# Turning the value product of an attention stage round, with V stationary and two heads in two column halves

## The chip, the cores and the metric

The kernel runs on one core of one Trainium2 chip. The metric is the device time of one launch in microseconds, the median of several runs. A core has a matrix engine (TensorE), three engines for elementwise work (VectorE, ScalarE, GpSimd), a DMA-issuing engine (SyncE) and 16 DMA engines. The engines run in parallel and wait for each other on semaphores. TensorE writes its results to PSUM, which has eight banks of 128 partitions x 512 fp32 words; here each bank is a tensor `bank[0]` to `bank[7]`.

## The reference

A trunk of two decoder layers over 512 tokens of width 1024, all in fp32. Layer 0 mixes tokens by sliding-window attention (window 128, 16 query heads of width 64 on 4 key/value heads, one learned sink logit per head), layer 1 by forgetting attention (16 heads, causal, with a bias c[t] - c[s] on the logits). Each is followed by a mixture of 16 experts of which each token uses two. Cut to the part that matters:

```
# layer 0, per head h and block of 128 queries; layer 1 without sink, over all earlier keys
scores = q @ k.T * 64**-0.5            (masked; layer 1: + c[q] - c[k])
probs  = softmax([scores, sink])[..., :-1]
out    = probs @ v                     # 64 columns per head
mix    = concat(out over heads) @ w_o
x      = layer_norm(alpha * x + mix)
```

## The kernel before

Each engine has its own instruction stream, written out by hand; order across engines comes only from named semaphores (`eng.wait_ge(S(name), n)`). Weights come through a ring of four slots in SBUF, loaded by SyncE. Plain fp32 matmuls are used for attention; the projections use three fp32r matmuls each (lines 523 to 525), with operands split in a high and a low part.

The attention of a layer works on 8 pairs of heads (`hp`). A pair has four steps, one for each block of 128 queries `n`, in the order 0, 3, 1, 2 (`N_ORDER`), so a layer has 32 steps `s`. In layer 0 block 0 sees one key tile of 128 keys and the others two; in layer 1 block n sees n + 1 tiles. `half` is the head within the pair. A step consists of:

- `scores(s)` on TensorE (line 618): Q times K for both heads. Head 0's operands lie in partitions 0 to 63 and head 1's in 64 to 127. In layer 1 a bf16 matmul adds the causal mask (line 624).
- `mask_and_max(s, half)` on VectorE (lines 1201 and 1208): adds the bias, scales, takes the maximum and writes to `sp` in SBUF.
- `expo(s, half)` on ScalarE (line 913): the exponential, with the row sums accumulated into `rsum` (the accumulator's read-out is a second record of the line).
- `turn_probs(s)` on TensorE (line 635): one transpose per key tile and head, head 0 into bank 3, head 1 into bank 4.
- `evac_probs(s)`: copies the transposed probabilities to `pT`, head 0 by ScalarE (line 927), head 1 by VectorE (line 1225). There is one `pT` for each head, so the copy of step s waits for the value product of step s - 1.
- `mix(s)` on TensorE (line 652): the value product. The transposed probabilities (128 x 128) are stationary, 64 columns of V move; the output is queries x head width in bank 5 or 6, by the pair's parity.

TensorE's order is, for each s: `turn_probs(s)`, `mix(s - 1)`, `scores(s + 2)`. ScalarE's is `expo(s + 1, 0)`, `evac_probs(s)`, `expo(s + 1, 1)`, and, in some steps, a cast of output weights (line 933). VectorE's is `evac_probs(s)`, then `mask_and_max(s + 2, ...)` for both heads.

A pair ends in the steps of the next one. VectorE's `normalise` (lines 1233 to 1240) adds the sinks in layer 0, takes the reciprocal of the sums and multiplies the pair's bank by it into `heads_out`. TensorE's `turn_out` transposes that back into the same bank (line 660), ScalarE's `out_high_part` writes the high part (line 938) and VectorE's `evac_out` the low part (line 1247) of the operand of the output projection.

Of the kernel before, what the change touches and what calls it, by code (L numbers as in the profile page):

```python
# [11 lines left out]
P = 128  # L12
SEQ, D = 512, 1024
HD = 64
# [34 lines left out]
def trunk(nc, x, ln_gain, ln_bias, swa_w_in, swa_sinks, swa_w_o, fox_w_in, fox_b_f, fox_w_o,  # L49
# [8 lines left out]
    with ctx:  # L58
# [48 lines left out]
        pT = area(14336, 2 * SEQ, "p (b n) -> p b n", b=2)  # L107
        heads_out = area(15360, 2 * SEQ, "p (b n) -> p b n", b=2)
        rtmp = area(16384, 2 * 8 * ROT, "p (a n) -> p a n", a=2)
# [364 lines left out]
        def _(eng):  # L474
# [35 lines left out]
            for l in range(DEPTH):  # L510
# [116 lines left out]
                def turn_probs(s):  # L627
                    hp, n = STEP[s]
                    k0, k1 = keys(n)
                    for half in range(2):  # L630
                        eng.wait_ge(S("exp_done"), 2 * STEPS * l + 2 * s + half + 1)
                        if s >= 1:
                            eng.wait_ge(S(f"pT_ready{half}"), STEPS * l + s)
                        for i in range(k1 - k0):
                            mm = eng.transpose(bank[3 + half][:, i * P:(i + 1) * P],  # L635
                                               sp[:, 2 * (s % 2) + half, i * P:(i + 1) * P], ident[:, :])
                        mm.then_inc(S("pT_done"), 1)

                def mix(s):
                    hp, n = STEP[s]  # L640
                    k0, k1 = keys(n)
                    if s % NT == 0:
                        if hp >= 2:
                            eng.wait_ge(S("aT_ready"), PAIRS * l + hp - 1)
# [189 lines left out]
        def _(eng):  # L834
# [31 lines left out]
            for l in range(DEPTH):  # L866
# [39 lines left out]
                def expo(s, half):  # L906
# [3 lines left out]
                    if s >= 2 * NT and s % NT == 0 and half == 0:  # L910
                        eng.wait_ge(S("o_ready"), PAIRS * l + hp - 1)
                    p = sp[:, 2 * (s % 2) + half, 0:nk]
# [8 lines left out]
                def evac_probs(s):  # L921
                    hp, n = STEP[s]
                    nk = P * (min(n, 1) + 1) if l == 0 else P * (n + 1)
                    eng.wait_ge(S("pT_done"), 2 * STEPS * l + 2 * s + 1)
# [10 lines left out]
                def out_high_part(hp):  # L935

                    eng.wait_ge(S("oT_done"), PAIRS * l + hp + 1)
                    eng.copy(attn_high[:, hp, :], bank[5 + hp % 2][:, :]).then_inc(S("aT_high"), 1)

                expo(0, 0)  # L940
                expo(0, 1)
                for s in range(STEPS):
# [9 lines left out]
                    if s >= NT and s % NT == 2:  # L952
                        out_high_part(s // NT - 1)
                out_high_part(PAIRS - 1)

# [110 lines left out]
        def _(eng):  # L1066
# [52 lines left out]
            for l in range(DEPTH):  # L1119
# [68 lines left out]
                def mask_and_max(s, half):  # L1188
# [4 lines left out]
                    if s >= 2:  # L1193
                        eng.wait_ge(S("pT_done"), 2 * STEPS * l + 2 * (s - 2) + half + 1)
                    if s >= 2 * NT and s % NT == 0 and half == 0:
# [23 lines left out]
                def evac_probs(s):  # L1219
                    hp, n = STEP[s]  # L1220
                    nk = P * (min(n, 1) + 1) if l == 0 else P * (n + 1)
                    eng.wait_ge(S("pT_done"), 2 * STEPS * l + 2 * s + 2)
                    if s >= 1:
                        eng.wait_ge(S("pv_done"), 2 * STEPS * l + 2 * (s - 1) + 2)
                    eng.tensor_copy(pT[:, 1, 0:nk], bank[4][:, 0:nk]).then_inc(S("pT_ready1"), 1)

                def normalise(hp):

                    eng.wait_ge(S("exp_done"), 2 * STEPS * l + 2 * NT * (hp + 1))
                    rs = rsum[:, hp % 2, :, :]  # L1230
                    if l == 0:
                        eng.wait_ge(S("sink_exp"), hp + 1)
                        link(eng.tensor_tensor(esink[:, hp % 2, :, :], esink[:, hp % 2, :, :], rs, ALU.add))
                        rs = esink[:, hp % 2, :, :]
                    ri = rinv[:, hp % 2, :, :]
                    link(eng.reciprocal(ri, rs))
                    eng.wait_ge(S("pv_done"), 2 * STEPS * l + 2 * NT * (hp + 1))
                    if hp >= 2:
                        eng.wait_ge(S("oT_done"), PAIRS * l + hp - 1)
                    eng.tensor_tensor(heads_out[:, hp % 2, :].rearrange("p (n h d) -> p n h d", n=NT, h=2),  # L1240
                                      bank[5 + hp % 2][:, :].rearrange("p (n h d) -> p n h d", n=NT, h=2),
                                      ri.unsqueeze(3).to_broadcast([P, NT, 2, HD]), ALU.mult).then_inc(S("o_ready"), 1)

                def evac_out(hp):

                    eng.wait_ge(S("aT_high"), PAIRS * l + hp + 1)
                    eng.tensor_tensor(attn_low[:, hp, :], bank[5 + hp % 2][:, :],
                                      attn_high[:, hp, :], ALU.subtract).then_inc(S("aT_ready"), 1)
# [19 lines left out]
                normalise(PAIRS - 1)  # L1268
                evac_out(PAIRS - 1)


# [247 lines left out]
```

## Time and profile before

| | |
|---|---|
| time, median of 3 runs | 946.85 us (946.28 to 947.75) |
| the profiled execution's own time | 946.05 us |
| its span | 944.3 us |
| TensorE matmuls, busy | 892.6 us, 95% of the span |
| VectorE, busy | 540.1 us, 57% |
| ScalarE, busy | 377.1 us, 40% |
| GpSimd, busy | 125.9 us, 13% |
| attention of layer 0, about | 91 to 159 us of the span |
| attention of layer 1, about | 574 to 663 us of the span |

The profile is of one execution; times within it count from the start of the span. An fp32 matmul shows as two records on TensorE and two weight loads, an fp32 transpose as one. Records of TensorE overlap, since matmuls are pipelined: a group's span is shorter than the sum of its durations. The chain is the work that ended last, followed back from the last instruction.

### The profile page before, as it was taken

What the parts mean: (1) busy time and instruction counts of PE and PEld (TensorE: products, weight loads), DVE (VectorE), ACT (ScalarE), POOL (GpSimd) and SP (SyncE); (2) the same over time, 40 slices, a digit from 0 to 9 for tenths busy, and PEclk for the clock granted to TensorE, in tenths of its full rate; (3) what the DMA queues carried; (4) which work ended last, traced back from release to release, by engine and by line L of the source; (5) the groups of instructions that cost most, each with busy time, mean ns of one, the idle gap of its engine ahead of it and who ended that gap; (6) DMA issues with size and microseconds to landing.
All of it is one profiled execution on the core that took longest, in us unless ns stands there. A gap on an engine that the chain in (4) does not pass through costs nothing.

```text
span 944.3 us, 12318 instructions
## 1 busy us (share of the span) xinstructions
PE 892.6 (95%) x4438; PEld 628.0 (67%) x4438; DVE 540.1 (57%) x1098; ACT 377.1 (40%) x755; POOL 125.9 (13%) x137
## 2 busy tenths in 40 slices
PE   5999999998999999989999999999999999999982
PEld 4887777884656656437878886887785566566530
DVE  3544886557776776475332224666356767667437
ACT  3322886001555555231132225777201355555300
POOL 2000332112010000041000001222111200100031
PEclk9999999998999999999999999999999999999997
DMA  9942000118999997663053222110117999999162
GB/s 314 359 171 89 2 2 1 41 48 326 355 388 377 394 390 271 213 222 137 0 185 129 90 90 108 49 47 23 67 45 281 313 373 384 394 378 368 34 212 89
DMA packets 49509, 183.14 MB, mean 194 GB/s; under 512 B 6496, under 2 KB 6496, under 8 KB 41264
## 3 DMA queue, kind: packets, MB, share of 16 engines
q1 hardware_dynamic: 35520, 132.34, 37.1%
q0 software_dynamic: 9200, 33.33, 10.8%
q10 hardware_dynamic: 4736, 16.78, 4.6%
q8 instruction: 31, 0.51, 0.2%
q14 instruction: 22, 0.18, 0.1%
HBM read 159.60 MB, written 22.84 MB: 193 GB/s over the span
## 4 chain that ended last, share of the span: by engine, by line
PE 88%; DVE 5%; DMA 3%; issue 2%; POOL 1%; ACT 1%; POOLq 0%; SPq 0%; DVEq 0%; ACTq 0%
PE bank L523 17%; PE bank L524 17%; PE bank L525 17%; PE bank L769 12%; PE bank L652 6%; PE bank L618 4%; PE bank L635 3%; PE bank L738 3%; PE bank L478 3%; PE bank L504 2%; PE bank L492 1%; PE bank L687 1%; DMA arena<-ys,pos 1%; PE bank L660 1%; DMA ring<-in_swa_w_in 1%
## 5 line engine op out<-in xcount | busy, mean ns | idle before, releaser
L1277 DVE TENSOR_TENSOR gu_low<-ring,gu_high 128x1024 fp32r<-128x1024 f32 x128 | 151.2, 1222 | 53.5 <-ACT gu_high L965 53.5
L965 ACT CAST gu_high<-ring 128x1024 fp32r<-128x1024 f32 x128 | 127.7, 1049 | 18.7 <-DVE arena L1412 17.6
L769 PE MATMUL bank<-ring,arena 128*96 128x512 f32 x256 | 115.8, 595 | 3.0 <-DVE arena L1402 1.8
L523 PE MATMUL bank<-gu_high,rows_high 128*96 128x512 f32 x256 | 112.3, 439 | 2.5 <-DVE rows_low L1396 2.5
L524 PE MATMUL bank<-gu_low,rows_high 128*96 128x512 f32 x256 | 101.0, 394 | 0.0
L525 PE MATMUL bank<-gu_high,rows_low 128*96 128x512 f32 x256 | 100.4, 392 | 0.0
L913 ACT ACTIVATE arena<-arena,nmax 128x256 f32<-128x256 f32 (+3 forms) x128 | 66.8, 522 | 31.0 <-DVE nmax L1208 20.2
L769 PEld LDWEIGHTS bank<-ring,arena 128*96 128x96 f32 x256 | 39.6, 165 | 55.5 <-issue 55.2
L523 PE MATMUL bank<-high,x_high 128*128 128x512 f32 x160 | 65.2, 408 | 6.9 <-DVE low L1104 5.4
L426 POOL TENSOR_TENSOR low<-ring,high 128x512 fp32r<-128x512 f32 x32 | 40.7, 1270 | 230.6 <-ACT high L933 230.6
L652 PE MATMUL bank<-arena 128*128 128x64 f32 x544 | 68.1, 269 | 0.2 <-ACT arena L927 0.2
L652 PEld LDWEIGHTS bank<-arena 128*128 128x128 f32 x544 | 65.8, 192 | 0.5 <-ACT arena L927 0.5
L524 PE MATMUL bank<-low,x_high 128*128 128x512 f32 x160 | 64.1, 401 | 0.0
L525 PE MATMUL bank<-high,xlow 128*128 128x512 f32 x160 | 63.9, 399 | 0.0
L523 PEld LDWEIGHTS bank<-gu_high,rows_high 128*96 128x96 f32 x256 | 41.4, 162 | 26.1 <-issue 7.2
L441 POOL DMA_INDIRECT arena<-xd,row_ids x32 | 29.2, 912 | 219.7 <-PE bank L738 193.6
L524 PEld LDWEIGHTS bank<-gu_low,rows_high 128*96 128x96 f32 x256 | 41.3, 161 | 22.9 <-issue 7.5
L525 PEld LDWEIGHTS bank<-gu_high,rows_low 128*96 128x96 f32 x256 | 41.3, 161 | 18.1
L478 PE MATMUL bank<-ident_b 128*128 128x512 bf16 x210 | 51.2, 403 | 1.3 <-ACT arena L997 1.3
L523 PE MATMUL bank<-high,attn_high 128*128 128x512 f32 x128 | 50.9, 398 | 0.0
L523 PE MATMUL bank<-x_high,wsplit 128*128 128x512 f32 x128 | 50.8, 397 | 0.0
L524 PE MATMUL bank<-xlow,wsplit 128*128 128x512 f32 x128 | 50.8, 397 | 0.0
(207 smaller groups left out, 1490.0 us busy)
## 6 DMA issues: line engine op xcount, KB each, us to landing
ring<-in_w_gate SPq DMA_DIRECT2D x32, 1024.0 KB, 12.5
ring<-in_w_up SPq DMA_DIRECT2D x32, 1024.0 KB, 14.7
ring<-in_w_down SPq DMA_DIRECT2D x32, 1024.0 KB, 14.9
ys<-arena ACTq DMA_DIRECT2D x32, 384.0 KB
ring<-in_fox_w_in SPq DMA_DIRECT2D x6, 2048.0 KB, 9.4
ring<-in_swa_w_in SPq DMA_DIRECT2D x3, 2048.0 KB, 10.6
ring<-in_swa_w_o SPq DMA_DIRECT2D x2, 2048.0 KB, 14.0
xd<-xres ACTq DMA_DIRECT2D x8, 512.0 KB, 2.6
```

The costliest lines, as they stand in the source:

```text
L426: eng.tensor_tensor(low, w, high, ALU.subtract).then_inc(S(f"out_low{l}"), 1)
L441: eng.indirect_dma_start(xe[0:CAP, e % RING, :], None, xd, bass.IndirectOffsetOnAxis(ap=row_ids[:, e:e + 1], axis=0)).then_inc(S(f"xe_in{l ...
L478: eng.matmul(bank[b][:, :], ident_b[:, :], ident_b[:, :].unsqueeze(1).to_broadcast([P, NT, P]), start=True, stop=True)
L523: eng.matmul(out, ah, wh, start=(c == 0), stop=False)
L524: eng.matmul(out, ah, wl, start=False, stop=False)
L525: return eng.matmul(out, al, wh, start=False, stop=(c == KC - 1))
L618: mm = eng.matmul(s_bank(s, half)[:, 0:nk], QT[r, hp, n * P:(n + 1) * P], KT[r, kp, k0 * P:k1 * P], start=True, stop=(l == 0))
L652: mm = eng.matmul(bank[5 + hp % 2][:, at:at + HD], pT[:, half, i * P:(i + 1) * P], (V0 if l == 0 else V)[:, k0 + i, v:v + HD], start=(i == ...
L769: mm = eng.matmul(bank[5 + half][0:CAP, :], hT[:, b, c, :], w[:, c, half * BLK:(half + 1) * BLK], start=(c == 0), stop=(c == FC - 1))
L913: eng.activation(p, p, ACT.Exp, bias=nmax[:, hp % 2, n, half:half + 1], scale=-1.0, accum_out=rsum[:, hp % 2, n, half:half + 1]).then_inc( ...
L965: eng.copy(gu_high[u % 2][:, :, part, :], slot_gate_up(use)[:, :, part, :]).then_inc(S("gu_high"), 1)
L1277: eng.tensor_tensor(gu_low[use % RING][:, :, part, :], slot_gate_up(use)[:, :, part, :], gu_high[u % 2][:, :, part, :], ALU.subtract).then ...
```

## The change

The operands of the value product change places: V (128 keys x 64) is stationary, and 128 columns of transposed probabilities move. The output is head width x queries. Head 0 goes to partitions 0 to 63 and head 1 to 64 to 127 of the same bank, so one pair's bank already has the layout that the output projection needs, and `turn_out` and `heads_out` go away. The loops are exchanged: key tiles outside, the two heads inside.

The division must now be by a value that differs per column. The reciprocals (`rinv`, queries on partitions) are spread by eight fp32 matmuls with the identity (`spread_sums`) into unused columns of the transposes' banks 3 and 4, in the first step of the next pair. ScalarE and VectorE copy them to `shares` (`take_shares`), and `divide` multiplies the pair's bank by them. The high and low parts are then made from `shares` in SBUF, no longer from PSUM. `normalise` is split in `sums`, now ahead of the masks in a pair's last step, and `divide`.

```diff
 def turn_probs(s):                                   # TensorE
...
                         if s >= 1:
                             eng.wait_ge(S(f"pT_ready{half}"), STEPS * l + s)
+                        if s > NT and s % NT == 1:
+                            eng.wait_ge(S(f"shares_here{half}"), PAIRS * l + s // NT)
                         for i in range(k1 - k0):
                             mm = eng.transpose(bank[3 + half][:, i * P:(i + 1) * P],
                                                sp[:, 2 * (s % 2) + half, i * P:(i + 1) * P], ident[:, :])
+                        if s >= NT and s % NT == 0:
+                            if half == 0:
+                                eng.wait_ge(S("sums_ready"), PAIRS * l + s // NT)
+                            mm = spread_sums(s // NT - 1, half)
                         mm.then_inc(S("pT_done"), 1)
+                def spread_sums(hp, part):
+                    for n in ((0, 1, 2), (3,))[part]:
+                        at = P * (1 + n % 3)
+                        for half in range(2):
+                            mm = eng.matmul(bank[3 + part][HD * half:HD * half + HD, at:at + P],
+                                            rinv[:, hp % 2, n, half:half + 1].to_broadcast([P, HD]), ident[:, :],
+                                            start=True, stop=True)
+                    return mm
 def mix(s):
...
-                    for half in range(2):
-                        eng.wait_ge(S(f"pT_ready{half}"), STEPS * l + s + 1)
-                        v = HD * (2 * hp // (NH // NKV) if l == 0 else 2 * hp + half)
-                        at = HD * (2 * n + half)
-                        for i in range(k1 - k0):
-                            mm = eng.matmul(bank[5 + hp % 2][:, at:at + HD], pT[:, half, i * P:(i + 1) * P],
-                                            (V0 if l == 0 else V)[:, k0 + i, v:v + HD], start=(i == 0), stop=(i == k1 - k0 - 1))
-                        mm.then_inc(S("pv_done"), 1)
-                def turn_out(hp):
-                    eng.wait_ge(S("o_ready"), PAIRS * l + hp + 1)
-                    for n in range(NT):
-                        mm = eng.transpose(bank[5 + hp % 2][:, n * P:(n + 1) * P], heads_out[:, hp % 2, n * P:(n + 1) * P], ident[:, :])
-                    mm.then_inc(S("oT_done"), 1)
+                    for i in range(k1 - k0):
+                        for half in range(2):
+                            if i == 0:
+                                eng.wait_ge(S(f"pT_ready{half}"), STEPS * l + s + 1)
+                            v = HD * (2 * hp // (NH // NKV) if l == 0 else 2 * hp + half)
+                            mm = eng.matmul(bank[5 + hp % 2][HD * half:HD * half + HD, n * P:(n + 1) * P],
+                                            (V0 if l == 0 else V)[:, k0 + i, v:v + HD], pT[:, half, i * P:(i + 1) * P],
+                                            start=(i == 0), stop=(i == k1 - k0 - 1))
+                            if i == k1 - k0 - 1:
+                                mm.then_inc(S("pv_done"), 1)
...
-                    if s >= NT and s % NT == 1:
-                        turn_out(s // NT - 1)
                 mix(STEPS - 1)
-                turn_out(PAIRS - 1)
+                eng.wait_ge(S("sums_ready"), PAIRS * (l + 1))
+                for half in range(2):
+                    eng.wait_ge(S(f"pT_ready{half}"), STEPS * (l + 1))
+                    spread_sums(PAIRS - 1, half).then_inc(S("pT_done"), 1)
 def evac_probs(s):                                   # ScalarE
...
                     eng.copy(pT[:, 0, 0:nk], bank[3][:, 0:nk]).then_inc(S("pT_ready0"), 1)
+                    if s >= NT and s % NT == 0:
+                        take_shares(s // NT - 1)
+                def take_shares(hp):
+                    if hp >= 2:
+                        eng.wait_ge(S("aT_ready"), PAIRS * l + hp - 1)
+                    eng.copy(shares[:, hp % 2, 0:3 * P], bank[3][:, P:4 * P]).then_inc(S("shares_here0"), 1)
 def out_high_part(hp):
-                    eng.wait_ge(S("oT_done"), PAIRS * l + hp + 1)
-                    eng.copy(attn_high[:, hp, :], bank[5 + hp % 2][:, :]).then_inc(S("aT_high"), 1)
+                    eng.wait_ge(S("o_ready"), PAIRS * l + hp + 1)
+                    eng.copy(attn_high[:, hp, :], shares[:, hp % 2, :]).then_inc(S("aT_high"), 1)
 def evac_probs(s):                                   # VectorE
...
+                def take_shares(hp):
+                    if hp >= 2:
+                        eng.wait_ge(S("aT_high"), PAIRS * l + hp - 1)
+                    eng.tensor_copy(shares[:, hp % 2, 3 * P:4 * P], bank[4][:, P:2 * P]).then_inc(S("shares_here1"), 1)
-                def normalise(hp):
+                def sums(hp):
...
-                    link(eng.reciprocal(ri, rs))
+                    eng.reciprocal(rinv[:, hp % 2, :, :], rs).then_inc(S("sums_ready"), 1)
+                def divide(hp):
                     eng.wait_ge(S("pv_done"), 2 * STEPS * l + 2 * NT * (hp + 1))
-                    if hp >= 2:
-                        eng.wait_ge(S("oT_done"), PAIRS * l + hp - 1)
-                    eng.tensor_tensor(heads_out[:, hp % 2, :].rearrange("p (n h d) -> p n h d", n=NT, h=2),
-                                      bank[5 + hp % 2][:, :].rearrange("p (n h d) -> p n h d", n=NT, h=2),
-                                      ri.unsqueeze(3).to_broadcast([P, NT, 2, HD]), ALU.mult).then_inc(S("o_ready"), 1)
+                    for part in range(2):
+                        eng.wait_ge(S(f"shares_here{part}"), PAIRS * l + hp + 1)
+                    eng.tensor_tensor(shares[:, hp % 2, :], bank[5 + hp % 2][:, :], shares[:, hp % 2, :], ALU.mult).then_inc(S("o_ready"), 1)
...
                     evac_probs(s)
+                    if s % NT == NT - 1:
+                        sums(s // NT)
...
                     if s >= NT and s % NT == 0:
-                        normalise(s // NT - 1)
+                        divide(s // NT - 1)
```

## Rows read from the trace of the kernel before

**Rows 1.** The page's chain that ended last, by engine and by line.
```profile
PE 88%; DVE 5%; DMA 3%; issue 2%; POOL 1%; ACT 1%; POOLq 0%; SPq 0%; DVEq 0%; ACTq 0%
PE bank L523 17%; PE bank L524 17%; PE bank L525 17%; PE bank L769 12%; PE bank L652 6%; PE bank L618 4%; PE bank L635 3%; PE bank L738 3%; PE bank L478 3%; PE bank L504 2%; PE bank L492 1%; PE bank L687 1%; DMA arena<-ys,pos 1%; PE bank L660 1%; DMA ring<-in_swa_w_in 1%
```

**Rows 2.** The chain in layer 1, one pair: start us, us, what.
```profile
624.27 1.73 PE bank L652 x16
626.01 0.42 PE bank L618 x4
...
628.15 1.06 PE bank L618 x4
...
629.65 1.29 PE bank L652 x12
...
634.12 0.45 PE bank L660 x4
...
635.01 1.73 PE bank L652 x16
```

**Rows 3.** The chain in layer 0, one pair.
```profile
111.68 0.84 PE bank L652 x8
...
118.20 0.70 DVE arena L1240
118.95 0.66 PE bank L660 x4
...
120.04 0.84 PE bank L652 x8
```

**Rows 4.** Six pairs of layer 0: busy PE, PEld, DVE, ACT, POOL; clock, DMA.
```profile
103.32:153.47 50.15, 47.67 (x375) 38.37 (x374) 41.69 (x150) 41.07 (x145) 15.28 (x13) 1.00 0.01 2
```

**Rows 5.** Groups by shape in layer 1: shapes, count, busy us, mean ns, idle.
```profile
L913 ACT ACTIVATE arena<-arena,nmax 128x512 f32<-128x512 f32 x16 | 11.5, 722 | 7.6 <-DVE nmax L1208 7.6
L618 PE MATMUL bank<-arena 64*128 64x512 f32 x32 | 9.0, 641 | 0.0
L927 ACT COPY arena<-bank 128x512 f32<-128x512 f32 x8 | 4.7, 586 | 1.1 <-PE bank L652 0.5
```

**Rows 6.** Scores of four key tiles, to 628.15 and to 628.65: ns min/median/max, starts.
```profile
L618 PE MATMUL bank<-arena x2: 693/693/693, 628.1 to 628.1; 64*128 64x512 f32 x2
L618 PE MATMUL bank<-arena x4: 589/641/693, 628.1 to 628.6; 64*128 64x512 f32 x4
```

**Rows 7.** Timeline of layer 0: start us, us, engine, line, shapes, count.
```profile
113.44 1.00 PE L652 MATMUL bank<-arena 128*128 128x64 f32 x8
114.09 0.37 ACT L927 COPY arena<-bank 128x256 f32<-128x256 f32 x1
114.55 0.42 DVE L1225 COPY arena<-bank 128x256 f32<-128x256 f32 x1 [0.22 <-PE bank L652]
115.01 0.44 PE L635 MATMUL bank<-ident,arena 128*128 128x128 f32 x2
117.77 0.16 DVE L1233 TENSOR_TENSOR esink<-esink,rsum 128x8 f32<-128x8 f32 x1
117.97 0.20 DVE L1236 RECIPROCAL rinv<-esink 128x8 f32<-128x8 f32 x1
```

**Rows 8.** Timeline where projection matmuls pass to 16 stationary columns.
```profile
477.89 0.39 PE L525 MATMUL bank<-high,xlow 128*128 128x512 f32 x1
478.12 0.40 PE L523 MATMUL bank<-x_high,wf_parts 128*16 128x512 f32 x1
```

**Rows 9.** Timeline near the end of layer 0's attention.
```profile
153.96 0.37 ACT L927 COPY arena<-bank 128x256 f32<-128x256 f32 x1 [0.26 <-PE bank L652]
154.23 0.51 ACT L913 ACTIVATE arena<-arena,nmax 128x256 f32<-128x256 f32 x1
154.64 0.19 ACT L913 ACTIVATION_READ_ACCUMULATOR arena<-arena,nmax 128x1 f32 x1
154.96 0.20 PEld L635 LDWEIGHTS bank<-ident,arena 128*128 128x128 f32 x2 [0.31 <-ACT arena L913]
```

More of the change, by code:

```diff
@@ L107, in trunk @@
         pT = area(14336, 2 * SEQ, "p (b n) -> p b n", b=2)
-        heads_out = area(15360, 2 * SEQ, "p (b n) -> p b n", b=2)
+        shares = area(15360, 2 * SEQ, "p (b n) -> p b n", b=2)
         rtmp = area(16384, 2 * 8 * ROT, "p (a n) -> p a n", a=2)
@@ L643, in mix @@
                         if hp >= 2:
-                            eng.wait_ge(S("aT_ready"), PAIRS * l + hp - 1)
+                            eng.wait_ge(S("o_ready"), PAIRS * l + hp - 1)
                         elif l == 0:
                             eng.wait_ge(S("qkT_free"), GROUPS[0] - 1 + hp)
-                    for half in range(2):
-                        eng.wait_ge(S(f"pT_ready{half}"), STEPS * l + s + 1)
-                        v = HD * (2 * hp // (NH // NKV) if l == 0 else 2 * hp + half)
-                        at = HD * (2 * n + half)
-                        for i in range(k1 - k0):
-                            mm = eng.matmul(bank[5 + hp % 2][:, at:at + HD], pT[:, half, i * P:(i + 1) * P],
-                                            (V0 if l == 0 else V)[:, k0 + i, v:v + HD], start=(i == 0), stop=(i == k1 - k0 - 1))
-                        mm.then_inc(S("pv_done"), 1)
-                def turn_out(hp):
-                    eng.wait_ge(S("o_ready"), PAIRS * l + hp + 1)
-                    for n in range(NT):
-                        mm = eng.transpose(bank[5 + hp % 2][:, n * P:(n + 1) * P], heads_out[:, hp % 2, n * P:(n + 1) * P], ident[:, :])
-                    mm.then_inc(S("oT_done"), 1)
+                    for i in range(k1 - k0):
[8 more added lines that the diff above has]
+                                mm.then_inc(S("pv_done"), 1)
                 if l == 0:
@@ L910, in expo @@
                     if s >= 2 * NT and s % NT == 0 and half == 0:
-                        eng.wait_ge(S("o_ready"), PAIRS * l + hp - 1)
+                        eng.wait_ge(S("sums_ready"), PAIRS * l + hp - 1)
                     p = sp[:, 2 * (s % 2) + half, 0:nk]
@@ L923, in evac_probs @@
                     nk = P * (min(n, 1) + 1) if l == 0 else P * (n + 1)
-                    eng.wait_ge(S("pT_done"), 2 * STEPS * l + 2 * s + 1)
+                    eng.wait_ge(S("pT_done"), (2 * STEPS + 2) * l + 2 * s + 1)
                     if s >= 1:
@@ L953, in _ @@
                         out_high_part(s // NT - 1)
+                eng.wait_ge(S("pT_done"), (2 * STEPS + 2) * l + 2 * STEPS + 1)
+                take_shares(PAIRS - 1)
                 out_high_part(PAIRS - 1)
@@ L1193, in mask_and_max @@
                     if s >= 2:
-                        eng.wait_ge(S("pT_done"), 2 * STEPS * l + 2 * (s - 2) + half + 1)
+                        eng.wait_ge(S("pT_done"), (2 * STEPS + 2) * l + 2 * (s - 2) + half + 1)
                     if s >= 2 * NT and s % NT == 0 and half == 0:
@@ L1221, in evac_probs @@
                     nk = P * (min(n, 1) + 1) if l == 0 else P * (n + 1)
-                    eng.wait_ge(S("pT_done"), 2 * STEPS * l + 2 * s + 2)
+                    eng.wait_ge(S("pT_done"), (2 * STEPS + 2) * l + 2 * s + 2)
                     if s >= 1:
@@ L1225, in evac_probs @@
                     eng.tensor_copy(pT[:, 1, 0:nk], bank[4][:, 0:nk]).then_inc(S("pT_ready1"), 1)
-                def normalise(hp):
+                    if s >= NT and s % NT == 0:
+                        take_shares(s // NT - 1)
+                def take_shares(hp):
[3 more added lines that the diff above has]
+                def sums(hp):
                     eng.wait_ge(S("exp_done"), 2 * STEPS * l + 2 * NT * (hp + 1))
@@ L1234, in normalise @@
                         rs = esink[:, hp % 2, :, :]
-                    ri = rinv[:, hp % 2, :, :]
-                    link(eng.reciprocal(ri, rs))
+                    eng.reciprocal(rinv[:, hp % 2, :, :], rs).then_inc(S("sums_ready"), 1)
+                def divide(hp):
                     eng.wait_ge(S("pv_done"), 2 * STEPS * l + 2 * NT * (hp + 1))
-                    if hp >= 2:
-                        eng.wait_ge(S("oT_done"), PAIRS * l + hp - 1)
-                    eng.tensor_tensor(heads_out[:, hp % 2, :].rearrange("p (n h d) -> p n h d", n=NT, h=2),
-                                      bank[5 + hp % 2][:, :].rearrange("p (n h d) -> p n h d", n=NT, h=2),
-                                      ri.unsqueeze(3).to_broadcast([P, NT, 2, HD]), ALU.mult).then_inc(S("o_ready"), 1)
+                    for part in range(2):
+                        eng.wait_ge(S(f"shares_here{part}"), PAIRS * l + hp + 1)
+                    eng.tensor_tensor(shares[:, hp % 2, :], bank[5 + hp % 2][:, :], shares[:, hp % 2, :], ALU.mult).then_inc(S("o_ready"), 1)
                 def evac_out(hp):
                     eng.wait_ge(S("aT_high"), PAIRS * l + hp + 1)
-                    eng.tensor_tensor(attn_low[:, hp, :], bank[5 + hp % 2][:, :],
+                    eng.tensor_tensor(attn_low[:, hp, :], shares[:, hp % 2, :],
                                       attn_high[:, hp, :], ALU.subtract).then_inc(S("aT_ready"), 1)
@@ L1264, in _ @@
                     if s >= NT and s % NT == 0:
-                        normalise(s // NT - 1)
+                        divide(s // NT - 1)
                     if s >= NT and s % NT == 2:
                         evac_out(s // NT - 1)
-                normalise(PAIRS - 1)
+                eng.wait_ge(S("pT_done"), (2 * STEPS + 2) * l + 2 * STEPS + 2)
+                take_shares(PAIRS - 1)
+                divide(PAIRS - 1)
                 evac_out(PAIRS - 1)
```

## The prediction

> **What bounds the kernel now.** I read the page's chain first: TensorE carries 88% of it, the value product (L652) 6% and the output transposes (L660) 1% [rows 1]. So the change acts in two stretches only, the attention of each layer. I name the steps of a head pair by their query block in running order: a (block 0), b (3), c (1), d (2). They hold 1, 4, 2, 3 key tiles in layer 1 and 1, 2, 2, 2 in layer 0.
>
> The chain of layer 1 repeats every 10.74 us and consists almost wholly of TensorE [rows 2]. The value product takes 1.73 us for 16 records, 0.107 us each; each fp32 matmul is two records, so a key tile (both heads) costs 0.43, a pair's ten tiles 4.27 us. Scores cost 0.42 for one key tile and 1.06 for four, 0.21 a tile and 0.21 fixed. The output transposes are 0.45.
>
> Layer 0 repeats every 8.36 us [rows 3]. Its chain runs once a pair through VectorE: `normalise` 0.70, then the output transposes 0.66, with TensorE waiting. TensorE is busy 47.67 of 50.15 us by records that overlap, ScalarE 41.07 and VectorE 41.69; the granted clock is 1.00, the 2.4 GHz level [rows 4]. Both helpers are near full, so the question in layer 0 is the latency of a loop, not TensorE's work.
>
> **The value product.** Turned round, it streams 128 columns of probabilities per record where it streamed 64. The scores show what fp32 streams cost: of four 512-column records two start together at 628.1 and two at 628.6 [rows 6], one of each pair in either row half, and the four take 1.06 us [rows 2]. Less the fixed 0.21 that is 0.43 for a record, two at a time; each lasts 0.64 with its latency [rows 5]. So a 128-column record streams for 0.107 us, and two heads in separate halves of the array can overlap. If column halves do that as row halves do, a key tile costs 2 x 0.107 = 0.21 in place of 0.43: 2.13 us less in layer 1 and 1.49 less in layer 0 of TensorE's time per pair. If they do not, it stays 0.43. No row shows a column pair; row halves are the nearest and I take overlap. The Trainium skill, TensorEngine Tiling (Array Packing), "When to Use Tiling", describes this swap with 2x column tiling as up to 2x; no run here shows it.
>
> **Switches.** In layer 0 the product's eight records start at 113.44, and the last stops streaming near 114.24. Then come the scores of two key tiles (0.43 of streaming) and two transposes from 115.01, 0.44 us in all where one lasts 0.27: the second started at 115.17, so the first streamed from about 115.06 [rows 7]. 0.83 less 0.43 leaves 0.20 for each change between whole array and half tiles. Inside whole-array work the spacing leaves 0.05. The change puts new boundaries of this sort between transposes and product in a, b and c (+0.15 each) and three around the two parts of `spread_sums` in d (+0.5). Against it: a 16-column matmul in fp32r follows a 128-column one after 0.23 us, the ordinary spacing [rows 8]; that bounds the price from below at nothing. The scores are fp32 like the new work and genuinely overlap, so I take 0.20. The same page of the Trainium skill, TensorEngine Tiling (Array Packing), "Key Properties", says that changing the tiling mode drains TensorE: by that rule the price is paid, in agreement with the scores' rows.
>
> **The sums.** Eight matmuls with 128 streamed columns replace four transposes: 4 x 0.21 = 0.85 us in place of 0.45. ScalarE gets a 384-column copy (0.38 of issue time by its slope below), VectorE a 128-column one (0.21). `sums` now stands before two masks, 0.2 us more for them in layer 1 and 0.4 in layer 0; the masks have over 0.5 us of slack, but the spreading waits for it, and behind the waiting TensorE stand the second head's transposes, the second part and product d, for which both copies wait. In b the transposes also wait for the shares' copy on ScalarE (0.28 + 0.14 + 0.48 + 0.15 = 1.05 after product d), but for the exponential longer still. `divide`, `out_high_part` and `evac_out` keep their sizes and lie beside TensorE's work, as `aT_ready` is needed a pair later. No transfer moves.
>
> **The loop that takes over.** ScalarE copies step s's probabilities only after step s-1's value product, and the exponential of the second head of s+1 is queued behind that copy; TensorE needs it for its transposes, and they precede product s. Before, the copy started when the first head's product was done, half a product early. Interleaved, both heads end together: the copy waits for the whole product. The loop from end to end of products:
> 0.28 (product end to copy: 113.44 + 3 x 0.107 + 0.05 = 113.81 to 114.09 [rows 7]), the copy, the exponential with its read-out, 0.20 (exponential end 154.83 to a transpose streaming at about 155.03; its weight load starts at 154.96 [rows 9]), the second head's transposes (0.05 and 0.11 per further tile), a switch of 0.20, the product at 0.21 a tile.
> A copy occupies ScalarE 0.27 for 256 columns (153.96 to 154.23 [rows 9]) and 0.49 for 512 (0.586 less the 0.10 by which neighbours overlap [rows 5]), so 0.11 a tile. The exponential is 0.60 for 256 columns (154.23 to 154.83 [rows 9]), 0.82 for 512 (0.72 - 0.09 + 0.19 [rows 5, 9]).
>
> Layer 0: b and c: 0.28 + 0.27 + 0.60 + 0.20 + 0.16 + 0.20 + 0.43 = 2.14 each. a: 0.28 + 0.14 + 0.38 (the shares' copy, ahead of the exponential) + 0.60 + 0.20 + 0.16 + 0.20 + 0.21 = 2.17. d: spreading waits for VectorE: 0.38 till its copy starts (it first finishes `evac_out`), 0.35 copy (0.42 less overlap), 0.20 the sum with the sinks and 0.20 reciprocal [rows 7], 0.20 to TensorE: 1.33; then 0.64, 0.20, 0.05, 0.20, 0.21, and the product 0.43: 3.06. Sum 9.5 us against 8.36: +1.2 a pair. What the removed wait for `normalise` gives (about 1.1) is in that difference; the waits for the sums and for ScalarE take its place.
>
> Layer 1: a 0.28 + 0.14 + 0.38 + 0.82 + 0.20 + 0.38 + 0.20 + 0.21 = 2.61; b 0.28 + 0.49 + 0.60 + 0.20 + 0.16 + 0.20 + 0.85 = 2.78; c 0.28 + 0.27 + 0.71 + 0.20 + 0.27 + 0.20 + 0.43 = 2.36. In d TensorE itself is the bound: from the end of the product to the next one was 1.50 (628.15 to 629.65 [rows 2]), plus 0.05, the sums' 0.85, switches 0.5, product 0.64: 3.54. Sum 11.3 against 10.74: +0.55 a pair.
>
> Seven pairs a layer: 8.1 + 3.9. The first pair has no sums: +0.6 in layer 0, and -0.7 in layer 1, where it loses only the 0.45 of transposes before but 1.3 of sums and 0.38 of ScalarE's copy after. At each layer's end a 0.70 `normalise` and 0.66 of transposes go, 0.85 of sums and a switch come, and the loop is longer: about -0.2 each. Total +11.5 on the profiled execution's 946.05: 957.5; the median stands 0.8 above that execution, so 958.
>
> **Rivals.**
> The nearest is that halves overlap and whole-to-column switches are free, as the 16-column rows would have it. Then each loop above loses 0.15 and d loses 0.5 (0.3 in layer 0): 8.8 and 10.35 a pair, +0.4 and -0.4. With -1.3 for layer 1's first pair and -0.5 at each end it comes to -2: about 944. For it: [rows 8]; against it: the scores' 0.20. It decides once a switch costs under about 0.04.
> Second, the intended one, on the other side: ScalarE's queue slips less than I think, because the first head's product still ends well before the second's or copy and exponential overlap, and TensorE stays the bound. Then layer 1 saves 2.13 + 0.45 - 0.85 = 1.7, less 0.95 of switches: 0.8 a pair. Layer 0 saves 1.49 + 0.45 - 0.85 - 0.95 = 0.1 and up to 1.0 of the wait for `normalise`: 1.1 a pair. With the ends 16 us: 930. Against it: the copy and the exponential stand in one in-order queue, and 113.44 to 114.09 shows the copy starting only when its product is done.
> Third, the change does not do what it says: column halves run one after the other. Key tiles stay at 0.43 and the sums cost 1.7: 1.49 + 0.85 and 2.13 + 0.85 a pair more than the sum above, 16 pairs, 42 us: 1000. For it: both column halves stream from the same 128 partitions, which row halves do not, and no row here has two such streams.
> The Trainium skill's TensorEngine Tiling (Array Packing), "PSUM Bottleneck", says that the copy out of PSUM may become the bottleneck once TensorE is faster; here that would be the main case's loop, whose copies the profile already has in line.
>
> **Numbers.** Main case 0.60, its own range 951 to 966 (two uncertain hand-overs of 0.05 in each of 64 loops, and 0.107 of fill in each group of column work if the second head starts a record late: up to +8). Free switches 0.10; TensorE stays the bound 0.12; one after another 0.18. The range 943 to 972 holds the main case, its edges and the free switches; 930 and 1000 are left outside with somewhat over 2 in 10. What a measurement can tell from no change is 0.2%, 1.9 us, so faster is under 945: 0.12, most of the free switches and some of the main case's error, 0.22; same 0.08; slower 0.70.
>
> **What would show it.** L652's replacement in pairs of starts, with durations near 0.33 us and a key tile each 0.21. Gaps of about 0.2 between transposes and product. TensorE idle 0.3 to 0.6 us a step, released by the exponential (L913's successor), and in d of layer 0 by the reciprocal. Pairs of 9.5 and 11.3 us. I am wrong if a key tile takes 0.43 (then 1000), if transposes and product follow at 0.05 (944), or if ScalarE's copy begins before the product's last record is near its end (930).

## The result

The changed kernel takes 951.89 us (median of 7, 949.48 to 955.32) against 946.67 for the one before: 1.0057 times, 95% interval 1.0037 to 1.0078. Slower was forecast and slower it is, but by 5.2 us (the interval is 3.5 to 7.4) where 11.5 were forecast.

The page's chain of the changed kernel, by engine and by line, beside [rows 1]:
```profile
PE 87%; DVE 4%; DMA 3%; issue 2%; ACT 1%; POOL 1%; POOLq 0%; DVEq 0%; SPq 0%
PE bank L523 17%; PE bank L524 17%; PE bank L525 17%; PE bank L781 12%; PE bank L637 4%; PE bank L668 3%; PE bank L618 3%; PE bank L750 3%; PE bank L650 2%; PE bank L478 2%; PE bank L504 2%; PE bank L492 1%; DMA arena<-ys,pos 1%; PE bank L699 1%; DMA ring<-in_swa_w_in 1%
```
The product (now L668) fell from 6% to 3%, the output transposes are gone, and the spreading (L650) takes 2%. TensorE's product did get short, and the kernel got slower. The chain of a pair in layer 1 shows both, beside [rows 2]:
```profile
620.19 1.02 PE bank L668 x16
621.22 0.42 PE bank L618 x4
621.64 0.22 PE bank L624 x2
621.86 1.02 PE bank L637 x6
622.88 0.59 PE bank L668 x8
623.47 1.06 PE bank L618 x4
...
624.86 0.81 PE bank L650 x12
625.67 0.26 PE bank L637
625.93 0.37 PE bank L650 x4
...
631.13 1.02 PE bank L668 x16
```
Four key tiles take 1.02 us where they took 1.73: 16 records of 0.107, two at a time, are 0.85, and 0.17 is a switch. But six transposes of step c (0.66 in full flow) now take 1.02, since the second head's three wait for the exponential, and step d holds 1.44 us of spreading and switches, with one transpose of the second head (0.26) among them. The pair is 10.94 us long; it was 10.74.

The timeline of layer 0, steps b and c, beside [rows 7] (L925 is the exponential, L939 ScalarE's copy, L1247 VectorE's copy, L637 the transposes, L1237 the subtraction for the sinks):
```profile
112.30 0.51 ACT L925 ACTIVATE arena<-arena,nmax 128x256 f32<-128x256 f32 x1
...
112.71 0.19 ACT L925 ACTIVATION_READ_ACCUMULATOR arena<-arena,nmax 128x1 f32 x1
...
112.95 0.20 PEld L637 LDWEIGHTS bank<-ident,arena 128*128 128x128 f32 x2 [0.23 <-ACT arena L925]
...
113.32 0.66 PE L668 MATMUL bank<-arena 128*64 128x128 f32 x8
...
113.49 1.27 POOL L426 TENSOR_TENSOR low<-ring,high 128x512 fp32r<-128x512 f32 x1 [3.79 <-ACT high L953]
113.54 1.23 DVE L1237 TENSOR_TENSOR esink<-nmax,sink 128x8 f32<-128x8 f32 x1
...
114.07 0.37 ACT L939 COPY arena<-bank 128x256 f32<-128x256 f32 x1 [0.15 <-PE bank L668]
...
114.70 0.41 DVE L1247 COPY arena<-bank 128x256 f32<-128x256 f32 x1
...
115.23 0.20 PEld L637 LDWEIGHTS bank<-ident,arena 128*128 128x128 f32 x2 [0.47 <-ACT arena L925]
115.26 0.41 PE L637 MATMUL bank<-ident,arena 128*128 128x128 f32 x2 [0.27 <-DVE arena L1247]
```
Three things are to be read here. ScalarE's copy starts at 114.07, 0.27 after the whole product stopped streaming (113.32 + 0.05 + 0.43). The exponential's read-out ends at 112.90, and the weight load of the second head's transposes starts at 112.95. And VectorE's subtraction of eight columns lasts 1.23 us and ends with GpSimd's operation (113.54 + 1.23 = 114.77; 113.49 + 1.27 = 114.76), so VectorE's copy is late and step c's transposes wait for it: the copy ends at 115.11, and their weight load starts at 115.23.

The lengths of the steps, each from one start of the scores to the next (worked out from the timelines' rows of L618; a step is named by the product that ends in it), in us:

| | d | a | b | c | pair |
|---|---|---|---|---|---|
| layer 0, before | 1.84 | 1.61 | 2.98 | 1.93 | 8.36 |
| layer 0, forecast | 3.06 | 2.17 | 2.14 | 2.14 | 9.5 |
| layer 0, changed | 2.87 | 2.09 | 2.03 | 2.28 | 9.27 |
| layer 1, before | 2.79 | 2.13 | 3.68 | 2.14 | 10.74 |
| layer 1, forecast | 3.54 | 2.61 | 2.78 | 2.36 | 11.3 |
| layer 1, changed | 3.48 | 2.52 | 2.69 | 2.25 | 10.94 |

Step b gains 0.95 to 0.99, from the wait for `normalise`, the output transposes and the four-tile product. The three others lose more than that: 1.86 us in layer 0 and 1.19 in layer 1.

### The profile page after: what moved, and what is told of

Same layout as the page of the kernel before. It is cut to its first block, busy times and chain, and to the rows that moved or that the text cites. A ratio compares the mean times of both kernels' runs of the same rounds, so it can differ in the third digit from the quotient of the medians.

```text
span 953.3 us, 12740 instructions
## 1 busy us (share of the span) xinstructions
PE 898.8 (94%) x4630; PEld 602.9 (63%) x4630; DVE 547.1 (57%) x1114; ACT 383.1 (40%) x771; POOL 125.5 (13%) x137
## 4 chain that ended last, share of the span: by engine, by line
PE 87%; DVE 4%; DMA 3%; issue 2%; ACT 1%; POOL 1%; POOLq 0%; DVEq 0%; SPq 0%
PE bank L523 17%; PE bank L524 17%; PE bank L525 17%; PE bank L781 12%; PE bank L637 4%; PE bank L668 3%; PE bank L618 3%; PE bank L750 3%; PE bank L650 2%; PE bank L478 2%; PE bank L504 2%; PE bank L492 1%; DMA arena<-ys,pos 1%; PE bank L699 1%; DMA ring<-in_swa_w_in 1%
## 5 line engine op out<-in xcount | busy, mean ns | idle before, releaser
L925 ACT ACTIVATE arena<-arena,nmax 128x256 f32<-128x256 f32 (+3 forms) x128 | 66.9, 524 | 12.7 <-DVE nmax L1230 10.1
L637 PE MATMUL bank<-ident,arena 128*128 128x128 f32 x272 | 54.5, 291 | 7.9 <-ACT arena L939 3.1
L525 PE MATMUL bank<-high,attn_low 128*128 128x512 f32 x128 | 50.9, 398 | 0.0
```

What stands on the lines that cost most here:

```text
L525: return eng.matmul(out, al, wh, start=False, stop=(c == KC - 1))
L637: mm = eng.transpose(bank[3 + half][:, i * P:(i + 1) * P], sp[:, 2 * (s % 2) + half, i * P:(i + 1) * P], ident[:, :])
L925: eng.activation(p, p, ACT.Exp, bias=nmax[:, hp % 2, n, half:half + 1], scale=-1.0, accum_out=rsum[:, hp % 2, n, half:half + 1]).then_inc( ...
```

## The experiments

**The heads outside, the key tiles inside.** Does the overlap come from neighbours in different column halves?
```diff
-for i in range(k1 - k0):
-    for half in range(2):
+for half in range(2):
+    for i in range(k1 - k0):
```


> The changed kernel with the two loops of the value product put back: heads outside, key tiles inside. Theory (the two heads' streams overlap because neighbouring matmuls lie in different column halves): head 0's matmuls now follow one another in one half and cannot overlap, so a key tile costs 0.43 us again in place of 0.21; a pair of layer 1 goes from 10.94 to about 12.2 us, one of layer 0 from 9.27 to about 9.95, together some 15 us over the changed kernel, 967. Rival (the halves don't overlap at all and the shorter product comes from the 64-column weight load): the product keeps its length, and as head 0 then ends early, ScalarE's copy starts earlier; 950 or less.

951.80 us, 1.0056 (1.0035 to 1.0077): no different from the changed kernel, and both expectations fell. Its chain in layer 1:
```profile
621.74 0.59 PE bank L668 x8
...
625.16 0.92 PE bank L668 x12
...
627.97 0.37 PE bank L668 x4
...
630.00 1.51 PE bank L668 x16
```
Less the switch of about 0.16 the first, third and fourth are 4, 2 and 12.6 times 0.107 us, for two, one and four key tiles. The second, three tiles, follows the spreading, which is in column halves too, so no switch lies before it: 8.6 times. Full overlap would be 4, 2, 8 and, for three tiles, 6; none at all would be twice that. The loss begins where a head has more than four records (two tiles): three tiles lose about 2.6 record times and four about 4.6. The starts of the single records say how: with eight records of each head, head 1's first starts at 630.42, beside head 0's fourth from the end (630.41); with six of each it is 625.21 beside 625.21. That is what it would be if a column half took up to four records ahead of their turn, and 0.5 record times were lost at the start. Layer 0, with two tiles at most, loses nothing. Layer 1's pair is 11.08 us (scores at 620.36 and 631.44), 0.14 longer only: b and d, with four and three tiles, are 0.48 and 0.27 longer, but head 0's copy starts earlier, and c and a are 0.35 and 0.27 shorter. The next run tests the reading of the four records.

**Blocks of two tiles.** The order is two tiles of head 0, the same two of head 1, then the next two of each.
```diff
-for i in range(k1 - k0):
-    for half in range(2):
+for first in range(0, k1 - k0, 2):
+    for half in range(2):
+        for i in range(first, min(first + 2, k1 - k0)):
```


> The changed kernel with the product in blocks: two key tiles of head 0, the same two of head 1, then the next two of each. Theory from the run with the heads outside (each column half takes up to four records ahead of its turn, so a head's four records may stand together without loss, and more may not): full overlap, step b of layer 1 as in the changed kernel, 2.69 us, pairs of 10.94. Rival (only direct neighbours in the order overlap, and the heads-outside order lost less for another reason): four key tiles take at least 0.2 us more, pairs of 11.1 or more.

952.18 us, 1.0047 (1.0030 to 1.0065). Its chain has
```profile
624.61 0.70 PE bank L669 x12
...
629.44 1.07 PE bank L669 x16
```
1.07 us for four tiles against 1.02 and 1.51: the overlap is whole, but for 0.05 us, with four records of a head together. The pair is 10.94 us as forecast; step b is 2.74, not 2.69.

**The exponential ahead of the copy.** The theory's main test, in ScalarE's queue:
```diff
     expo(s + 1, 0)
+    expo(s + 1, 1)
     evac_probs(s)
-    expo(s + 1, 1)
```


> The changed kernel with one exchange in ScalarE's queue: the exponential of the second head of step s+1 ahead of the copy of step s, not behind it. Theory (the loop product, copy, exponential, transposes bounds steps a, b and c of both layers): the loop is cut, TensorE's own work and the copies are left: about 10.25 us a pair in layer 1 (from 10.94) and 8.45 in layer 0 (from 9.27), some 12 us less than the changed kernel: 940. Rival (TensorE bounds the changed kernel by its switches and the sums, the loop only runs beside): no change beyond 2 us, 950 to 952.

944.84 us, 0.9981 (0.9971 to 0.9991) times the kernel before, 7 us under the changed one: the loop was a bound, and not TensorE beside it. 12 us were expected. Steps a went from 2.09 to 1.88 and from 2.52 to 2.31, b in layer 1 from 2.69 to 2.53, c in layer 0 from 2.28 to 2.02; b of layer 0 and c of layer 1 stayed at 2.03 and 2.25, and pairs are 8.78 and 10.58 us instead of 8.45 and 10.25. The timeline of this kernel's layer 1 shows what took the loop's place in c:
```profile
623.62 0.56 DVE L1229 CUSTOM_DVE_ANT_0 arena<-bank,lnp 128x384 f32<-128x384 f32 x1 [0.21 <-PE bank L624]
...
624.01 1.09 PE L668 MATMUL bank<-arena 128*64 128x128 f32 x16
...
624.11 0.55 DVE L1229 CUSTOM_DVE_ANT_0 arena<-bank,lnp 128x384 f32<-128x384 f32 x1
...
624.84 0.60 ACT L925 ACTIVATE arena<-arena,nmax 128x384 f32<-128x384 f32 x1
...
625.47 0.37 ACT L939 COPY arena<-bank 128x256 f32<-128x256 f32 x1
...
625.99 0.52 PE L637 MATMUL bank<-ident,arena 128*128 128x128 f32 x3 [0.24 <-ACT arena L939]
```
Now the copy stands behind both exponentials, and these behind both masks on VectorE. The product had stopped streaming at 624.01 + 0.05 + 0.85 = 624.91, so the copy could have started near 625.18 and started at 625.47. The gain in c of layer 0 is no witness for ScalarE's loop: in the changed kernel that step waited for VectorE's late copy, as shown above.

**The same in the kernel before.** Its copies and exponentials stand in the same order:
```diff
     expo(s + 1, 0)
+    expo(s + 1, 1)
     evac_probs(s)
-    expo(s + 1, 1)
```

> The same exchange in the kernel before. Theory: in layer 1 TensorE is the bound there (its chain has nothing else), so pairs stay at 10.74 us; in layer 0 ScalarE's loop was just short of TensorE's pace, so at most 0.2 us a pair: 945 to 947 in all. Rival (ScalarE's order is bad for any form of the product, and the change to the product has no part in it): several us less here as well, 940 or under.

948.81 us, 1.0026 (1.0014 to 1.0037): slower, which neither expected. The same new wait costs here and buys nothing: in layer 0 step b is 0.14 shorter and a 0.15 longer, so the pair stays at 8.36, and in layer 1 a goes from 2.13 to 2.48. Its timeline in layer 1, whose pair is 11.08 us instead of 10.74:
```profile
618.37 0.69 DVE L1207 CUSTOM_DVE_ANT_0 arena<-bank,lnp 128x512 f32<-128x512 f32 x1
...
619.21 0.71 ACT L913 ACTIVATE arena<-arena,nmax 128x512 f32<-128x512 f32 x1
...
619.91 0.24 ACT L927 COPY arena<-bank 128x128 f32<-128x128 f32 x1
...
620.30 1.07 PE L635 MATMUL bank<-ident,arena 128*128 128x128 f32 x8 [0.17 <-ACT arena L927]
```
So the gain of the exchange goes with the short product: in the kernel before, the loop did not set the length of a pair in either layer.

**The spreading after both heads' transposes.** Two switches fewer:
```diff
-    [transposes head 0] [sums_ready] spread_sums(hp, 0)
-    [transposes head 1]              spread_sums(hp, 1)
+    [transposes head 0] [transposes head 1]
+    [sums_ready] spread_sums(hp, 0); spread_sums(hp, 1)
```


> The changed kernel with the order transposes of head 0, transposes of head 1, then both parts of the spreading, where it was transposes, part, transposes, part. Two changes between whole array and column halves fall away, and head 1's transposes run while TensorE waits for the reciprocal. Theory (each such change costs 0.15 to 0.2 us and step d is bound by TensorE itself): 0.35 us a pair in layer 1 and 0.45 in layer 0, 14 pairs, 5.5 us less: 946. Rival (changes to column halves are free): nothing in layer 1, 0.1 us a pair in layer 0, so 951.

948.92 us, 1.0015 (1.0002 to 1.0028), 3 us under the changed kernel; 5.5 were expected. In layer 1 step d went from 3.48 to 3.18: 0.30 for two switches, 0.15 each, near the 0.35 expected. In layer 0 it went from 2.87 to 2.69, 0.18 and not 0.45, as TensorE there waits for the reciprocal in either order, and c remained the 2.28 of VectorE's late copy.

**Each spreading matmul twice.**
```diff
-for half in range(2):
+for half in (0, 1, 0, 1):
```


> The changed kernel with each matmul of the spreading issued twice (the same values written again), everything else as it is. Theory (column halves overlap, and the sums lie bare on TensorE's path in step d and at the end of each layer): 0.85 us more a pair, 16 pairs, 13.6 us over the changed kernel: 965. If the halves ran one after the other it would be 1.7 us a pair, 979. Rival (the sums lie beside other waits and cost little): under 5 us, 957 or less.

966.86 us, 1.0203 (1.0180 to 1.0226): 15 us over the changed kernel. The pairs are 10.15 and 11.81 us instead of 9.27 and 10.94, 0.87 to 0.88 more each. The sums' 0.85 us lies bare on the path, and the halves overlap there too:
```profile
621.22 1.46 PE bank L650 x24
...
622.94 0.59 PE bank L650 x8
```

**ScalarE's casts of output weights in other steps.** GpSimd's operation follows each cast. First in a and c, then in a and d:
```diff
-if s % 2 == 1:
+if s % 2 == 0:                # casts_even;  casts_ad: s % NT in (0, NT - 1)
     out_weights_high(s // 2)
```


> The changed kernel with ScalarE's casts of the output weights in steps a and c (even steps), where they were in b and d; GpSimd's subtraction follows each cast. Theory (in layer 0 VectorE's small subtraction for the sinks, 1.23 us for eight columns where it was 0.66 before the change, only waits for GpSimd's 1.27 us operation to end, and holds up the copy of step c): the subtraction takes under 0.7 us, step c of layer 0 goes from 2.28 to about 2.05 us, 1.6 us in all: 950. Rival (it is slow by itself): it stays at 1.23 wherever GpSimd works.

> The changed kernel with ScalarE's casts of the output weights in steps a and d, so that GpSimd's subtraction falls neither on the sinks' subtraction (step b) nor on the low part's (step c). Theory (VectorE's operations with both sources in SBUF wait for GpSimd's): step c of layer 0 2.04 us (from 2.28), step d as in the changed kernel; 1.9 us less, 950. Rival (the casts themselves are what hurts): slower, towards the 963.7 of the casts in a and c.

In a and c: 963.69 us, 1.0176 (1.0158 to 1.0193), 12 us slower, though the expected part happened: the small subtraction took 0.17 us, and step c of layer 0 2.04. But step d became 4.06 us there and 4.01 in layer 1. The subtraction in the groups by shape:
```profile
L1237 DVE TENSOR_TENSOR esink<-nmax,sink 128x8 f32<-128x8 f32 x8 | 1.3, 166 | 0.3
```
and the timeline of layer 0's step d:
```profile
115.39 0.60 ACT L953 CAST high<-ring 128x512 fp32r<-128x512 f32 x1
...
115.90 0.61 ACT L958 CAST attn_high<-arena 128x512 fp32r<-128x512 f32 x1
116.07 1.27 POOL L426 TENSOR_TENSOR low<-ring,high 128x512 fp32r<-128x512 f32 x1 [2.67 <-ACT high L953]
...
116.55 1.34 DVE L1277 TENSOR_TENSOR attn_low<-arena,attn_high 128x512 fp32r<-128x512 f32 x1 [1.01 <-ACT attn_high L958]
...
117.81 0.41 DVE L1247 COPY arena<-bank 128x256 f32<-128x256 f32 x1
```
Two things hold VectorE up there. ScalarE's cast of the weights (L953) now stands ahead of its cast of the high part (L958), so `evac_out` (L1277), which needs the high part, starts 0.74 us after product c's first record (115.81), where it started beside it in the changed kernel (115.58 beside 115.60); VectorE is idle for 1.01 us before it. Then it takes 1.34 us, 0.69 where GpSimd is still, since it meets GpSimd's operation. Both hold up the next copy: by these rows the meeting is 0.65 of the 1.19 us that the step grew by and the later start the rest; no run takes the two apart. The change had moved an operand of `evac_out` from PSUM to SBUF; the runs show the meeting only in that form. In a and d it meets neither: 949.79 us, 1.0029 (1.0016 to 1.0042), 2.1 to 2.8 us under the changed kernel for 1.9 expected, with the subtraction at 0.17, c at 2.04 and d at 2.89. The Trainium skill, SBUF — State Buffer, "SBUF: two separate sides", has VectorE and GpSimd share a port pair that one of them holds alone for a whole instruction, an operation of VectorE with two SBUF inputs included where GpSimd's reads SBUF. The traces agree: the small subtraction ended 0.02 to 0.03 us after GpSimd's operation, `evac_out` 0.55 after it, and `divide`, with one operand in PSUM, kept its 0.69 with GpSimd at work beside it.

**Together.** Both exchanges; then with the casts in a and c; then with the casts in a and d.

> The changed kernel with both exchanges: the second head's exponential ahead of the copy, and the spreading after both heads' transposes. Theory (they act on different steps: a, b, c the one, d the other): their gains add, 10.28 us a pair in layer 1 and 8.60 in layer 0; 3.4 us under the first exchange alone: 941.4. Rival (a single resource, ScalarE's or VectorE's work, now sets the pair's length): no more than the first alone, 944 to 945.

> Both exchanges and the casts in even steps. Theory of the held-up VectorE: another 1 to 2 us in layer 0, 940. Rival (with the exponentials ahead of the copy, a cast in step c delays ScalarE's later copy, which is the bound there): no gain or a loss over both exchanges alone, 941 to 944.

> Both exchanges and the casts in a and d. Theory: steps b and c of layer 0 1.9 us each (from 2.02), 1 to 2 us under both exchanges alone, 940.5. Rival (another wait on ScalarE or VectorE bounds these steps): 942.

941.95 us, 0.9951 (0.9933 to 0.9970): in the whole time the two gains add, as expected, though pairs are 8.41 and 10.40 us instead of 8.60 and 10.28. With the casts in a and c 947.43, 1.0012 (0.9998 to 1.0027), worse than without for the reason above, its step d at 3.39 in layer 0. With the casts in a and d 940.70, 0.9926 (0.9909 to 0.9943), the lowest median here and 0.7% under the kernel before; from the 941.95 without the casts' move it is not clear of the noise. Its pairs are 8.27 and 10.40 us; c of layer 0 is 1.88 as expected, b stayed at 2.02. In layer 1 its chain runs through ScalarE's queue in two places of each pair, one of them:
```profile
616.68 1.23 ACT arena L926 x3
...
618.21 0.15 ACT arena L940
618.35 0.38 ACT arena L948
...
618.87 1.07 PE bank L637 x8
```
These are the exponentials, the copy, the shares' copy, then eight transposes of TensorE.

**The changed kernel once more.**

> The changed kernel once more, beside the others: 950 to 953. Theory of the profiled execution (its 955.3 us held a stretch of 3 us at TensorE's lower clock at the end of layer 0's attention, which not every execution has): the pairs' lengths are the same, 9.27 and 10.94 us, whether the stretch is there or not.

952.60 us, 1.0058 (1.0045 to 1.0071), with the same pairs. In its profile layer 0's attention goes from the first scores to the first matmul of the output projection in 76.3 us (87.4 to 163.7); before it was 70.5 (88.2 to 158.7), in the first profile of the changed kernel 77.3 (88.4 to 165.7).

## Why the prediction was wrong

The direction, the place and the mechanism were right. Column halves overlap, two streams at a time. The loops through ScalarE bound steps a, b and c, but for c of layer 0: the exchange of exponential and copy took 0.21 us off a in each layer and 0.16 off b in layer 1. For b of layer 0 and c of layer 1, which kept their lengths because another wait took the loop's place, the loop rests on its sum and on the waits in the timelines. Whole-to-column switches cost 0.15 to 0.17 where 0.20 was taken, so the rival of free switches fell. So did the one of serial halves (a key tile is 0.21, not 0.43), and the intended one: the copy starts 0.27 after the product's end.

The term that was mis-sized is the loop's hand-over from the exponential to the transposes, 0.20 us. It was read where the transposes' weight load starts 0.13 after the exponential's end [rows 9]. In that place VectorE's copy, which they need too, ended at the same moment (154.42 + 0.42 = 154.84 beside 154.83), so the row could not say whom they waited for. Where the copy comes last, the weight load starts 0.12 after it (115.11 to 115.23 in the changed kernel); where the exponential comes last by itself, 0.05 after it (112.90 to 112.95). The trace of the kernel before had such a clean place, with the copy's end 0.38 us earlier:
```profile
93.31 0.42 DVE L1225 COPY arena<-bank 128x256 f32<-128x256 f32 x1 [0.19 <-PE bank L652]
...
93.92 0.19 ACT L913 ACTIVATION_READ_ACCUMULATOR arena<-arena,nmax 128x1 f32 x1
...
94.16 0.20 PEld L635 LDWEIGHTS bank<-ident,arena 128*128 128x128 f32 x2 [0.20 <-ACT arena L913]
```
The exponential ends at 94.11, the weight load starts at 94.16. To the first streaming it is about 0.06 more, 0.11 in all. With 0.10 in place of 0.20 the three loops come to 2.07, 2.04 and 2.04 in layer 0 (measured 2.09, 2.03, 2.28) and 2.51, 2.68 and 2.26 in layer 1 (2.52, 2.69, 2.25). Two smaller errors of the loop cancel: two transposes were charged 0.16 and stream for 0.21, and the switch was charged 0.20 and costs 0.15. The hand-over makes 0.30 us a pair, 14 pairs: 4.2 us of the 6.3 between forecast and result.

Two more terms were off and nearly cancelled. Layer 0's c was 0.24 over the corrected loop, since the sinks' subtraction had been given no wait for GpSimd, though it already lasted 0.66 before, four times what it needs. Layer 0's d was 0.19 under the forecast: the spreading streams from 1.16 after product c instead of 1.33 (117.19 + 0.05 against 115.60 + 0.05 + 0.43). VectorE's copy started 0.32 after the product and not 0.38, and the hand-over from the reciprocal to TensorE was 0.11, not 0.20. Layer 1's d, 3.54, measured 3.48. Over the whole stages the forecast was +8.5 and +3.0; in the profiles layer 0 is 5.8 longer (second profile) and layer 1, from the last projection group to the output projection, 0.5. What lies outside the seven repeating pairs came to -1.0 in layer 0 and -1.4 in layer 1, where +0.4 and -0.9 were forecast; no run takes these apart. The sum of 6.3 is 1.1 over the difference of the medians; the medians of the changed kernel's two series differ by 0.7 already, and the rest is open.

The chances have a slip of their own: the two cases left outside the range had 0.12 and 0.18, which is 0.30 and not somewhat over 2 in 10.

The likeliest case's own range, 951 to 966, held the time. What failed was the size of the loss, by a factor of two, and two thirds of that are a small latency that counts 42 times.

## What to carry to other kernels

When a change shortens one engine's work in a software pipeline, write down the loop that passes through the other engines' in-order queues and compare it with the new work, not the old: here the loop stood close to TensorE's pace already (at 94.16 the transposes of the kernel before waited for the exponential), and the signal that starts it came half a product later. A hand-over latency is to be read only where a single release explains the wait, since it is paid once a step; the trace of the kernel before held both sorts of place. And when an operand moves from PSUM to SBUF, look at what GpSimd is doing at that time.

## What was not expected of the hardware

A column half of TensorE took records ahead of their turn: with one head's records all before the other's, up to four records (two fp32 key tiles) of a head were no loss, twelve records took about 8.6 record times instead of 6 and sixteen 12.6 instead of 8. With blocks of two tiles sixteen took about 8.5. The count of four is read from these sizes and from where head 1's first record starts; how a half comes to hold four is not shown.

VectorE's subtraction of 128 x 8 elements took 0.17 us by itself, 0.66 or 1.23 with GpSimd at work, and its end fell on the end of GpSimd's operation, 0.02 to 0.03 us after it.

In the first profile of the changed kernel TensorE's granted clock fell to half, 1.2 GHz, at the end of layer 0's attention:
```profile
160.00:162.00 2.00, 1.14 (x14) 0.55 (x8) 1.54 (x3) 1.75 (x7) 1.11 (x1) 1.00 0.00 0
162.00:163.00 1.00, 0.61 (x9) 0.37 (x8) 0.87 (x2) 0.30 (x2) 0.00 (x0) 1.00 0.00 0
163.00:164.00 1.00, 0.88 (x11) 0.88 (x13) 0.46 (x3) 0.59 (x2) 0.34 (x1) 0.78 0.00 0
164.00:165.00 1.00, 1.00 (x14) 1.00 (x12) 0.00 (x0) 0.00 (x0) 0.93 (x1) 0.50 0.06 16
165.00:166.00 1.00, 1.00 (x8) 0.67 (x5) 0.18 (x1) 0.48 (x1) 0.00 (x0) 0.50 0.00 0
```
The columns are stretch, length, busy time of PE, PEld, DVE, ACT and POOL, clock, DMA share and GB/s. TensorE had been busy for 1.14 of 2 us and 0.61 of 1 us, waiting for the last two steps' copies; the last spreading then took 1.71 us instead of 0.85. The second profile has the same waits and a clock of 1.00 throughout this place, and so has the kernel before. Of the other profiles those of the spreading after both heads' transposes and of the casts in a and c have the same fall at this place. What decides it is open. It does not show as a wider scatter: the changed kernel's executions lie between 949.5 and 955.3, those of the kernel before between 944.1 and 949.7 in the longest series.
